# Two gate products of a gated recurrence cut into half blocks on the two row halves of TensorE

## The reference

```python
xb = xc.reshape(B, S, RNN_BLOCKS, RNN_BLOCK)          # 16 blocks of 64 channels
r = jax.nn.sigmoid(jnp.einsum('bshi,hij->bshj', xb, w_rg_a).reshape(B, S, C) + b_rg_a)
i = jax.nn.sigmoid(jnp.einsum('bshi,hij->bshj', xb, w_rg_x).reshape(B, S, C) + b_rg_x)
log_a = -LRU_C * r * jax.nn.softplus(-lru_lambda)
a = jnp.exp(log_a)
b = jnp.sqrt(-jnp.expm1(2.0 * log_a)) * (i * xc)
_, h = lax.associative_scan(_lin_rec_combine, (a, b), axis=1)
```

## Time and profile before

| what | value |
|---|---|
| median of three runs | 2462.28 us |
| the three runs | 2462.13, 2462.28 and 2466.03 us |
| the profiled execution | 2465.56 us, span 2463.8 us |
| PE busy | 2409.3 us, 98% of the span |
| DVE, ACT, POOL busy | 925.2, 822.7 and 985.9 us |
| mean granted TensorE clock | 0.99 of full |

### The profile page before, as it was taken

One profiled execution on the slowest core, in us unless ns is written; L12 is line 12 of the kernel. 1 busy time (PEld: TensorE's weight loads), 2 busy tenths in 40 slices (PEclk: granted clock), 3 DMA queues, 4 the chain that ended last, 5 costly groups with the idle time before them and its releaser, 6 DMA issues.

```text
span 2463.8 us, 28169 instructions
## 1 busy us (share of the span) xinstructions
PE 2409.3 (98%) x11092; PEld 1907.1 (77%) x11092; DVE 925.2 (38%) x1485; ACT 822.7 (33%) x1267; POOL 985.9 (40%) x426
## 2 busy tenths in 40 slices
PE   7899999999999999999999999999999999999996
PEld 4567677777888888887787778787878888888885
DVE  4764466566500620210555434343421412203113
ACT  5245444342322332222434333333332312213321
POOL 1344333234455534443333324242434444444552
PEclk9899999999999999999999999999999999999998
DMA  8962133235544343333222323232333444454332
GB/s 295 398 246 80 60 127 111 94 107 191 160 144 141 126 163 94 93 98 91 65 81 62 97 78 109 84 112 81 107 98 99 154 149 130 128 168 120 93 102 86
DMA packets 98435, 309.55 MB, mean 126 GB/s; under 512 B 10624, under 2 KB 12032, under 8 KB 98176
## 3 DMA queue, kind: packets, MB, share of 16 engines
q1 hardware_dynamic: 98304, 307.76, 39.1%
HBM read 285.69 MB, written 20.97 MB: 124 GB/s over the span
## 4 chain that ended last, share of the span: by engine, by line
PE 89%; DVE 5%; ACT 2%; issue 2%; DMA 1%; SPq 1%; POOL 0%; DVEq 0%; POOLq 0%; ACTq 0%
PE bank L535 24%; PE bank L538 24%; PE bank L536 24%; PE bank L531 2%; PE bank L534 2%; PE bank L532 2%; PE bank L1043 2%; PE bank L1067 1%; PE bank L1055 1%; DVE hlo L1725 1%; DMA raw<-in_wst 1%; PE bank L829 1%; PE bank L840 1%; DVE hlo L2445 1%; DMA rawx<-in_wst 1%
## 5 line engine op out<-in xcount | busy, mean ns | idle before, releaser
L2513 POOL TENSOR_TENSOR wlo<-raw,whi 128x1024 fp32r<-128x1024 f32 x365 | 896.5, 2461 | 1246.6 <-ACT whi L1160 1238.3
L535 PE MATMUL bank<-hhi,whi 128*128 128x512 f32 x2752 | 1089.1, 396 | 19.1 <-ACT whi L1160 16.5
L538 PE MATMUL bank<-hhi,wlo 128*128 128x512 f32 x2752 | 1078.7, 392 | 7.3 <-POOL wlo L2513 7.2
L536 PE MATMUL bank<-hlo,whi 128*128 128x512 f32 x2752 | 1076.5, 391 | 0.0
L535 PEld LDWEIGHTS bank<-hhi,whi 128*128 128x128 f32 x2752 | 518.9, 189 | 144.4 <-ACT whi L1160 18.1
L538 PEld LDWEIGHTS bank<-hhi,wlo 128*128 128x128 f32 x2752 | 518.9, 189 | 123.6 <-POOL wlo L2513 13.1
L536 PEld LDWEIGHTS bank<-hlo,whi 128*128 128x128 f32 x2752 | 519.4, 189 | 107.1 <-issue 0.7
L1160 ACT ACTIVATE whi<-raw 128x1024 fp32r<-128x1024 f32 x365 | 384.5, 1055 | 588.7 <-PE bank L538 482.7
L2321 DVE TENSOR_SCALAR S<-S,sm 128x512 f32<-128x512 f32 (+1 forms) x64 | 78.0, 1218 | 0.6
L534 PE MATMUL bank<-wlo,hhi 128*128 128x512 f32 x192 | 74.8, 390 | 1.1 <-POOL wlo L2513 1.1
L1590 ACT ACTIVATE S<-S,sm 128x512 f32<-128x512 f32 (+1 forms) x64 | 35.3, 551 | 119.0 <-DVE sm L2311 119.0
(11 more groups left out here) (308 smaller groups left out, 2104.3 us busy)
## 6 DMA issues: line engine op xcount, KB each, us to landing
raw<-in_wst SPq DMA_DIRECT2D x397, 512.0 KB, 3.6
rawx<-in_wst SPq DMA_DIRECT2D x54, 512.0 KB, 6.6
rawy<-in_wst SPq DMA_DIRECT2D x26, 512.0 KB, 4.6
tgs<-TS SPq DMA_DIRECT2D x32, 256.0 KB, 3.9
axr<-tgs SPq DMA_DIRECT2D x32, 256.0 KB, 4.0
X<-in_xt SPq DMA_DIRECT2D x4, 1024.0 KB, 14.4
pls<-stg SPq DMA_DIRECT2D x16, 256.0 KB, 9.3
axr<-in_xt SPq DMA_DIRECT2D x16, 256.0 KB, 2.8
```

The costliest lines, as they stand in the source:

```text
L535: e.matmul(o, hi, xh, start=first, stop=False)
L536: e.matmul(o, hi, xl, start=False, stop=False)
L538: return e.matmul(o, lo, xh, start=False, stop=last)
L2513: e.tensor_tensor(sub(wlo, PAIR[c], CH), slots[slot(c)], sub(whi, PAIR[c], CH).bitcast(F), ALU.subtract).then_inc(*up("wlo_pool", "wlo", c))
```

## The change

The stationary tile `lwt` shrinks from 128x256 to 128x128. Its rows 0 to 63 hold the first block's two gate matrices side by side (a, then x), its rows 64 to 127 the second block's in the other order (x, then a). One product takes rows 0 to 63 of `lwt` and `xc`, the other rows 64 to 127, so that each is 64 rows by 128 columns and gives both gates of one block, in a bank of its own. The tanh of a gate then has to be gathered from the two banks, 64 partitions from each: four instructions on ACT in place of two, and for the second gate (`g2`) the partitions are moved by 64 on the way. TensorE now waits for both banks before the first of the two products. The bank of each half is freed by the second gate's tanh. The next step on DVE waits for the last of the four.

```diff
-        lwt = at(M0 + 106, 256, F, "lwt")
+        lwt = at(M0 + 106, P, F, "lwt")
...
-                for j in range(2):
-                    o, prior = claim(ring("side"), "lru", c, j)
-                    w.wait_ge(*done("conv", c))
-                    w.wait_ge("lrw", 16 * (c + 1))
+                to = [claim(ring("side"), "lru", c, j) for j in range(2)]
+                w.wait_ge(*done("conv", c))
+                w.wait_ge("lrw", 16 * (c + 1))
+                for o, prior in to:
                     for f in prior:
                         w.wait_ge(*f)
-                    e.matmul(o[:, :], lwt[:, P * j:P * (j + 1)], xc[:, :], start=True, stop=True).then_inc(
+                for j, (o, prior) in enumerate(to):
+                    e.matmul(o[:, :], lwt[64 * j:64 * j + 64, :], xc[64 * j:64 * j + 64, :], start=True, stop=True).then_inc(
                         *up("lru_pe", "lru", c, j))
...
                 for j, (g_, hb) in enumerate(((g1, hba), (g2, hbx))):
-                    w.wait_ge(*done("lru", c, j))
-                    w.wait_ge(*done("terms"))
-                    if c:
-                        w.wait_ge(*done("scan", c - 1))
-                    e.activation(g_[:, :], bank("lru", c, j)[:, :], ACT.Tanh, scale=0.5, bias=hb[:, c:c + 1]).then_inc(
-                        *up("tanh_act", "gate", c, j, frees=("lru", c, j)))
-                w.wait_ge(*done("gate", c, 0))
+                    for hd in range(2):
+                        at, to = slice(64 * (hd ^ j), 64 * (hd ^ j) + 64), slice(64 * hd, 64 * hd + 64)
+                        w.wait_ge(*done("lru", c, hd))
+                        w.wait_ge(*done("terms"))
+                        if c:
+                            w.wait_ge(*done("scan", c - 1))
+                        e.activation(g_[to, :], bank("lru", c, hd)[at, :], ACT.Tanh, scale=0.5,
+                                     bias=hb[to, c:c + 1]).then_inc(
+                            *up("tanh_act", "gate", c, j, hd, frees=("lru", c, hd) if j else None))
+                w.wait_ge(*done("gate", c, 0, 1))
...
-                w.wait_ge(*done("gate", c, 1))
+                w.wait_ge(*done("gate", c, 1, 1))
...
-    lrw = np.zeros((8, P, 2, P), np.float32)
+    lrw = np.zeros((8, P, P), np.float32)
     for j, n in enumerate(("w_rg_a", "w_rg_x")):
         w = i[n][0]
-        lrw[:, 0:64, j, 0:64] = w[0::2]
-        lrw[:, 64:128, j, 64:128] = w[1::2]
+        lrw[:, 0:64, 64 * j:64 * j + 64] = w[0::2]
+        lrw[:, 64:128, 64 - 64 * j:128 - 64 * j] = w[1::2]
```

More of the change, by code:

```diff
@@ L2944 @@
         "cst": _constants(),
-        "lrw": lrw.reshape(8, P, 2 * P),
+        "lrw": lrw,
         "w2bd": w2bd.reshape(P, 2 * P),
```

## The result

| | before | changed |
|---|---|---|
| median, 20 runs each | 2461.97 us | 2465.97 us |
| lowest and highest | 2460.61 and 2466.03 us | 2464.22 and 2470.9 us |
| profiled execution (span) | 2465.56 us (2463.8) | 2466.64 us (2464.9) |

The ratio is 1.0016 with a 95% interval of 1.001 to 1.0022: the changed kernel is 4.0 us slower (2.5 to 5.4), which is inside the 0.2% (4.9 us) that I called no change and inside the wider range (2459.3 to 2467.0, 8 in 10). But it is 3.7 us above the forecast, 1.5 us above the end of the forecast's own range (2460.5 to 2464.5, chance 0.60), and clear of zero.

What follows compares the result with a forecast made beforehand. TensorE, busy 98% of the span, was taken as the bound except at two waits for gac. Saving -2.8, ACT delay +2.2 and clock +0.3 twice gave no change from the median: 2462.3 us, range 2460.5 to 2464.5, wider 2459.3 to 2467.0.

Steps and rivals of the forecast that it cites:

- The regimes: Gate-product stage: PE's time counts in six tiles; in two, after c = 3 and c = 7, ACT's lateness counts.
- race with POOL: After c = 3: DVE's last gac sum still starts before POOL's second wlo, by 0.3 us.
- second rival: At c = 3 the last gac sum falls behind POOL: +2.5 us there, 2464 to 2465 us in all; chance 0.15.
- Where PE binds: Gate-product stage: PE's saving counts in six tiles; after c = 3 and c = 7 the wait for gac swallows it.
- The saving on PE: Gate products, line 870: 1.25 us in place of 1.72, 0.46 saved a tile, 2.8 us over six tiles.
- ACT's four halves: Tanh on ACT: four steps of 0.58 us, line 1424 1.09 us later, adding 2.2 us over two tiles.
- The clock: TensorE at half clock after both gac waits: longer waits cost 0 to +1.7 us each, taken as +0.3 each.
- The sum: Whole kernel: -2.8 + 2.2 = -0.6 us, plus +0.3 for each of two waits at low clock: no change.
- side-by-side passes: Gate products on PE: the two 64-row products run together, starting within 0.01 us, as in lines 836 and 837.
- the cover in the other six tiles: Tiles other than c = 3 and 7: ACT's delay is hidden; at c = 1, 2.24 us of room against 1.55.
- the free transfer: Fetch of the half-size lwt: issued 19 us before it is needed, so its smaller size doesn't show.
- no new wait for a bank: Gate products on PE: waiting for two banks at once moves the second wait 0.86 us forward but costs nothing.

Runs made afterwards that it cites:

- a_two: Changed kernel with two whole-bank tanh in place of four, halves not gathered so gates are mixed up: 2458.69 us, ratio 0.9985 to before.
- early pairs: DVE's gac sums moved ahead into its wait for the gates, each kernel twice: changed 2449.36 and 2448.94 us, before 2451.26 and 2453.16 us.
- a_guard: Changed kernel with POOL's wlo at c = 3 made to wait for the fourth gac sum: 2465.44 us, ratio 1.0013 to before.
- b_halves: Kernel before, full products kept, each tanh split into two unmoved halves of 64 partitions: 2465.86 us, ratio 1.0016.
- a_order: Changed kernel with tanh halves reordered so reads start on the same partition inside each pair, writes and biases not: 2466.39 or 2466.35 us, as the changed one.
- a_write: Changed kernel with tanh halves reordered so writes and biases start on the same partition inside each pair, reads not: 2466.39 or 2466.35 us.
- b_order: Kernel before with unmoved tanh halves, ordered so reads and writes start on the same partition inside each pair: 2469.13 us, a single execution.

## Why the prediction came out as it did

The wider range held, and so did "no change within 0.2%"; that the kernel is slower, by 2.5 to 5.4 us, was not forecast. The regimes and most prices were right, but the forecast's own case did not come: its price for ACT's halves failed and took the race with POOL with it. What came is the second rival, put at 0.15, and at 2466.0 us it is 1 to 2 us dearer than was said (2464 to 2465). That the verdict still held is owed in part to luck, to a band of 0.2% that is wider than what these medians can tell apart. By the prediction's steps, with the stage in the two traces (+3.1 us):

- **Where PE binds.** Right: six tiles on PE, two over ACT and DVE, and the gain of PE in these two lost. `a_two` and the early pairs show both halves of it.
- **The saving on PE.** 0.46 us a tile forecast, 0.51 found; six tiles give -3.1 us for -2.8. Entering the 64-row form (0.09), the second passes (0.53 behind the first) and leaving it (0.53 to the transposes) cost what the pair of lines 836 and 837 showed; the transposes lose less on their first load (0.06) than the 0.10 taken from lines 535 and 536. "The transposes 1.25 to 1.26 us after the start" was a slip: by the sum's own terms that 0.10 falls behind their start, which leaves 1.15, as measured.
- **ACT's four halves.** The step that failed first: "The pace is 0.58 us from line 1420 to line 1424". That row is of two full-height instructions with the same starting partition, and I carried it over to halves whose start changes each time. They take 0.71. Line 1424's tanh comes 1.59 us later instead of 1.09. Without the blocked sum, line 879 follows by 1.55 us (12.65 us after M at c = 7, 11.10 before), so the two tiles pay 2 x 1.55 = 3.1 us instead of 2.2. I had bounded the delay above by +0.3 a half, so the range held it.
- **The race with POOL.** "It still gets in first, by 0.3 us" fell with the last step: four halves are 0.50 us slower than thought, and the sum comes 0.20 us too late. It costs 1.95 us (14.60 us from M to line 880 after c = 3, less 12.65 after c = 7; the `a_guard` run takes away as much). The rival had 2.5 us and a chance of 0.15. A margin of 0.3 us under a term whose upper bound was four times 0.3 was no margin, and the rival deserved a larger chance.
- **The clock.** Without waits the stretch from line 880 to the next products is 23.63 us and that after c = 7, to the `PT`x`V` products, 6.34 us (both early kernels). Before they are 26.99 and 8.10, in the changed kernel 27.12 and 9.11: 5.12 and 6.26 us lost to half clock. The low clock in the traces accounts for them: in the changed kernel PE works at half clock from 428.32 to 435.50 and from 559.64 to 565.20, and half of these 12.7 us is 6.4. The change adds 1.1 where I took 0.6. How the loss grows with the wait is open. Over the other traces the loss is 5.7 (`a_guard`), 5.5 (`b_halves`), 4.9 (`a_two`), 6.6 and 6.6 (`a_order`, `a_write`) and 6.0 (`b_order`): about 5 us with waits near 3 us, 5.5 to 6.6 with waits over 4. But two traces with the same waits (`b_halves`, `b_order`) differ by 0.5, and each is a single execution, so the size of this term is likely rather than shown.
- **The sum.** -3.1 + 3.1 + 1.95 + 1.1 = +3.1 us, the stage's difference. The medians say +4.0 (2.5 to 5.4); the 0.9 us between lie within the interval and no run attributes them.

Right without reserve were the side-by-side passes (both start within 0.01 us), the cover in the other six tiles, the free transfer, and no new wait for a bank.

## What to carry to other kernels

Before shortening work on the engine that binds, find the places where it waits for another: there the saving is lost, and what the edit adds to the other engine's chain is paid in full, so two such places outweighed six good ones. Here the cure was to move the late work into a hole of its engine, which was worth 12.7 us with the change and 8.5 to 10.7 without it. Test both halves of a change together as well as alone: here a race was lost only with both. Take the pace of a short instruction from a row with the same change of starting partitions, and where an ordering holds by a few tenths of a us, price both orders.

## What the runs showed of the hardware

- On ScalarE, a tanh of 64x512 from PSUM lasts as long as one of 128x512 (0.68 and 0.69 us here). The next one starts 0.10 us before it ends if it reads and writes from the same starting partitions, and 0.03 us after it if either start changes (0 to 64 or back; the bias moved with the written start).
- A VectorE instruction with two SBUF inputs that starts 0.20 us after one of GpSimd's ends only 0.54 us after GpSimd's does: 2.71 us for 0.75. When it starts 0.34 us before GpSimd's (`b_halves`), it takes its 0.75.
- Two 64-row fp32 products of 512 columns on the two row halves take 1.15 us where two of 128 rows take 1.72, switching in and out included; the transposes behind them lose another 0.06.
